# An expert layer whose VectorE instructions read the gathering tokens and a list of indices from PSUM, with fewer PSUM banks for the first products

## The reference, cut to what matters

```python
def block(hb):                       # 128 tokens
    q = (hb @ wq).reshape(128, 8, 2, 128)
    s = jnp.einsum('thsd,snd->thsn', q, subkeys)
    s1, i1 = lax.top_k(s[:, :, 0], 16)
    s2, i2 = lax.top_k(s[:, :, 1], 16)
    cand = (s1[..., :, None] + s2[..., None, :]).reshape(128, 8, 256)
    sc, ci = lax.top_k(cand, 16)
    e1 = jnp.take_along_axis(i1, ci // 16, axis=-1)
    e2 = jnp.take_along_axis(i2, ci % 16, axis=-1)
    idx = e1 * 128 + e2              # 16384 experts
    gate = jax.nn.softmax(sc, axis=-1)
    u_sel, v_sel = u_tab[idx], v_tab[idx]
    act = gelu(jnp.einsum('td,thkd->thk', hb, u_sel)) * gate
    return jnp.einsum('thk,thkd->td', act, v_sel)
```

## Time and profile before

| | us |
|---|---|
| median of 3 runs | 4457.77 (4456.28 to 4461.15) |
| span of the profiled execution | 4448.2 |
| median less span | 9.6 |
| PE busy | 4243.8 (95%) |
| DVE busy | 3101.9 (70%) |
| ACT busy | 1806.5 (41%) |
| POOL busy | 1550.2 (35%) |

### The profile page before, as it was taken

How to read it: one execution, slowest core, us unless ns; L and a number is a source line. 1 busy time by engine, 2 the same in 40 slices (tenths; PEclk the granted TensorE clock), 3 DMA queues, 4 the chain that set the end, 5 groups by cost and what they waited for, 6 DMA issues and landing times.

```text
span 4448.2 us, 66516 instructions
## 1 busy us (share of the span) xinstructions
PE 4243.8 (95%) x26227; PEld 3699.9 (83%) x26227; DVE 3101.9 (70%) x4740; ACT 1806.5 (41%) x2814; POOL 1550.2 (35%) x1005
## 2 busy tenths in 40 slices
PE   7979989999989999999999999999999999999998
PEld 5857745779989999999989877699889877877997
DVE  5866667559878988788878555588478544555873
ACT  4245411233334544333345335455255333323542
POOL 2044224215887657777721110211111110112121
PEclk8989999999999999999999999999999999999999
DMA  4133522224875779999933322133323332102332
GB/s 180 53 105 124 182 69 70 80 89 157 260 247 199 271 287 393 376 382 388 366 108 105 95 87 66 48 105 96 100 91 105 95 104 77 47 34 68 103 99 75
DMA packets 232190, 665.74 MB, mean 150 GB/s; under 512 B 22519, under 2 KB 88455, under 8 KB 229704
## 3 DMA queue, kind: packets, MB, share of 16 engines
q1 hardware_dynamic: 110528, 389.87, 26.1%
q0 software_dynamic: 38752, 142.90, 8.8%
q10 hardware_dynamic: 82600, 128.71, 8.1%
HBM read 593.24 MB, written 68.16 MB: 149 GB/s over the span
## 4 chain that ended last, share of the span: by engine, by line
PE 74%; DVE 16%; POOL 3%; ACT 3%; issue 3%; DMA 1%; ACTq 0%; DVEq 0%; POOLq 0%
PE ps L271 14%; PE ps L272 14%; PE ps L273 14%; PE ps L2727 5%; PE ps L2729 5%; PE ps L2728 5%; DVE r L240 2%; PE ps L1611 2%; DVE A L2042 2%; PE ps L3762 1%; PE ps L1690 1%; DVE A L2341 1%; POOL r L240 1%; DVE A L2342 1%; DVE r L290 1%
## 5 line engine op out<-in xcount | busy, mean ns | idle before, releaser
L271 PE MATMUL ps<-r,r 128*128 128x384 f32 (+1 forms) x3944 | 1454.4, 369 | 22.2 <-POOL r L240 14.6
L272 PE MATMUL ps<-r,r 128*128 128x384 f32 (+1 forms) x3944 | 1436.3, 364 | 0.0
L273 PE MATMUL ps<-r,r 128*128 128x384 f32 (+1 forms) x3944 | 1435.8, 364 | 0.0
L240 DVE TENSOR_TENSOR r<-A,r 128x1024 fp32r<-128x1024 f32 x436 | 603.9, 1387 | 718.7 <-ACT r L234 713.0
L234 ACT ACTIVATE r<-A 128x1024 fp32r<-128x1024 f32 x513 | 542.2, 1058 | 1200.9 <-PE ps L273 995.3
L271 PEld LDWEIGHTS ps<-r,r 128*128 128x128 f32 x3944 | 745.6, 189 | 118.7 <-issue 24.5
L272 PEld LDWEIGHTS ps<-r,r 128*128 128x128 f32 x3944 | 745.7, 189 | 81.5 <-issue 3.4
L273 PEld LDWEIGHTS ps<-r,r 128*128 128x128 f32 x3944 | 745.2, 189 | 81.6
L287 ACT ACTIVATE r<-A 128x512 fp32r<-128x512 f32 (+1 forms) x796 | 474.1, 611 | 503.4 <-DVE A L2415 233.5
L2727 PE MATMUL ps<-r,r 128*128 128x256 f32 x2128 | 601.0, 282 | 3.5 <-DVE A L2891 2.5
L2729 PE MATMUL ps<-r,r 128*128 128x256 f32 x2128 | 600.4, 282 | 0.0
(11 more groups left out here) (532 smaller groups left out, 5544.8 us busy)
## 6 DMA issues: line engine op xcount, KB each, us to landing
A<-in_pu SPq DMA_DIRECT2D x128, 512.0 KB
A<-in_pv SPq DMA_DIRECT2D x128, 512.0 KB
A<-in_f1i SPq DMA_DIRECT2D x88, 512.0 KB, 3.5
A<-in_f2i SPq DMA_DIRECT2D x88, 512.0 KB, 3.6
A<-in_w_in SPq DMA_DIRECT2D x48, 512.0 KB
acts<-A ACTq DMA_DIRECT2D x128, 192.0 KB
gates<-A ACTq DMA_DIRECT2D x8, 3072.0 KB, 11.3
A<-gates ACTq DMA_DIRECT2D x32, 768.0 KB
```

What stands on the lines that cost most here:

```text
L240: e.tensor_tensor(self.vr(at + 1024, 1024), self.v(self.st0 + 1024 * (u % RS), 1024), self.vr(at, 1024).bitcast(F32), ALU.subtract).then_i ...
L271: t.matmul(o, hi, xh, start=first and k == k0, stop=False)
L272: t.matmul(o, hi, xl, start=False, stop=False)
L273: m = t.matmul(o, lo, xh, start=False, stop=final and k == K - 1)
```

## The change

The gathering tokens stay in banks 6 and 7, where the transposes left them (the two are now one tensor of 1024 columns, `last2`), and DVE reads them there for rows 0 to 95 (`L.kept`). From row 96 on it reads the copy in SBUF as before, since vexp 6 and 7 want the banks: PE waits for row 95 before vexp 6. The transposes of the gates move from banks 6 and 7 to 3, 4 and 5, which need a wait for the last scores. Early products use banks 0, 1, 2 up to c = 69 and from there only 0 and 1 in turn. After the GELU of c = 70 ACT copies the list of indices into bank 2, and `hot_v` reads it there. In tiles and sizes nothing else changes.

```diff
-        self.PS = [ctx.enter_context(nc.psum_tensor(f"ps{i}", [128, 512], F32)) for i in range(8)]
+        self.PS = [ctx.enter_context(nc.psum_tensor(f"ps{i}", [128, 512], F32)) for i in range(6)]
+        self.last2 = ctx.enter_context(nc.psum_tensor("ps67", [128, 1024], F32))
+        self.PS += [self.last2[:, 0:512], self.last2[:, 512:1024]]
...
+        L.THREE = 70
...
+        L.bank = [c % 3 if c < L.THREE else (c + 1) % 2 for c in range(128)]
         for b in range(3):
-            self.plan([("early", c) for c in range(b, 128, 3)] + [("vsum", b)] + ([("sum t", b)] if b < 2 else []), (b,))
-            self.plan([("gates", i) for i in range(b, NT // 4, 3)] + [("vsum", 3 + b)], (3 + b,))
-        self.plan([("x tokens", 0), ("gate t", 1), ("gate t", 3), ("vsum", 6)], (6,))
-        self.plan([("x tokens", 1), ("gate t", 2), ("vsum", 7)], (7,))
+            self.plan([("early", c) for c in range(128) if L.bank[c] == b] + [("vsum", b)] + ([("sum t", b)] if b < 2 else []), (b,))
+        for b in range(3):
+            self.plan([("gate t", b + 1)] + [("gates", i) for i in range(b, NT // 4, 3)] + [("vsum", 3 + b)], (3 + b,))
+        for i in range(2):
+            self.plan([("x tokens", i)], (6 + i,))
+            self.plan([("vsum", 6 + i)], (6 + i,))
...
+        L.kept = L.steps["second", 4].stop
...
-                v.scalar_tensor_tensor(out=row, in0=row, scalar=1.0, in1=self.v(L.XT, 1024), op0=ALU.mult, op1=ALU.mult,
+                tokens = self.last2[:, :] if n < L.kept else self.v(L.XT, 1024)
+                v.scalar_tensor_tensor(out=row, in0=row, scalar=1.0, in1=tokens, op0=ALU.mult, op1=ALU.mult,
...
+                t.wait_ge(*S.at("out", "scores", 15))
                 ps = self.bank_t(t, "gate t", tt)
...
+            if c == L.THREE:
+                a.wait_ge(*S.at("out", "early", c - 2))
+                a.activation(self.PS[2][:, 0:128], self.cst("iota128"), ACT.Copy).then_inc(*S.on("a", "iota kept"))
...
-            io = self.cst("iota128").unsqueeze(1).to_broadcast([128, 8, 128])
+            io = self.PS[2][:, 0:128].unsqueeze(1).to_broadcast([128, 8, 128])
...
+        v.wait_ge(*S.at("iota kept"))
         v.wait_ge(*S.at("out", "gate t", 3))
...
+            if x == 6:
+                t.wait_ge(*S.at("row used", L.kept - 1))
```

## The result

| | us |
|---|---|
| before, median of 4 runs | 4457.02 (4451.72 to 4461.15) |
| changed, median of 4 runs | 4426.84 (4425.38 to 4446.54) |
| ratio | 0.994, 95% interval 0.9916 to 0.9963 |
| changed once more, median of 6 runs | 4430.25 (4425.62 to 4440.89), ratio 0.9939 (0.9919 to 0.9959) |

What follows compares the result with a forecast made beforehand. PE sets the end; POOL and DVE hold each other up when DVE reads two SBUF operands, and DVE limits the gates stage. 4457.8 - 12.2 - 9.7 + 1.6 + 0.4 = 4437.9 us; range 4429 to 4451.

Steps and rivals of the forecast that it cites:

- C: Rival: the change does not free POOL and DVE at this size, only costs are left; 4460 us, chance 0.07.
- A: Rival: POOL's gathers are slow for another reason, half the top-k gain goes; 4444 us, chance 0.10.
- B: Rival: DVE remains the limit in the gates stage, half of that gain; 4443 us, chance 0.12.
- D: Rival: weights late with two banks, GELUs hold PE in early 114 to 127; 4468 us, chance 0.07.
- both main terms: The gains from PE's shorter waits in the top-k stage (12.2 us) and the gates stage (9.7 us).
- a clock that would come back behind the large gap: Top-k stage: full clock would return another 3.4 us (17% of 20 us); counted only in the range's lower end.
- top-k stage: Rows read from PSUM let POOL keep pace; PE's 18.0 us of waits fall to 5.75, gain 12.2 us.
- gates stage: List and rows from PSUM make PE the limit; its 17.5 us of waits fall to 7.8, gain 9.7 us.
- wait at vexp 0: Early 127 and vexp 0 share bank 0, so PE waits for the GELU; cost 1.6 us.
- two banks: From c = 71 PE waits for the GELU of c - 2; cost 0.4 us, bounds 0 and 6.
- waits for ACT's copies: Gates stage: of 3.0 us of such waits 2 stay, since they hang on ACT's order.
- first gap: Start of the gates stage: PE stands 7.25 us behind POOL's remainder and first product; 5.8 us are left.

Runs made afterwards that it cites:

- both_sbuf: The changed kernel, with rows 0 to 95 and the comparisons reading tokens and list from SBUF again; 4456.88 us, ratio 0.9999 to the kernel before.

## Why the prediction was right

**The direction and the mechanism** held, each step of it. An instruction with one PSUM input was not held (the 96 rows took 1199 to 1222 ns), as L1642 had let expect. The table of the Trainium skill, "VectorE: DVE Perf Modes", section on the TRN2 errata, with its dearer PSUM input, is not borne out at 1024 columns either, for instructions with one input in PSUM and one in SBUF: 1.21 us, as with both in SBUF where nothing holds them. both_sbuf rules out that anything else made the gain. Against C: these rows and the comparisons were not held. Against A: gathers beside them went to 0.95 us. Against B: DVE left its limit. Against D: no GELU held PE in early 114 to 127.

**The size** came out larger: -19.9 forecast, by the layer's times -30.45 + 1.58 = -28.9 us. The ratio times the first median of before gives 4431 us, inside the range; the median itself, 4426.84, lies 2 us under its lower end, the second series' 4430.25 inside. So the range was met at its edge, and partly by luck: both main terms lie beyond their own bounds (13.3 and 11.7), and the end at 4429 was reached with 3.4 us for a clock that would come back behind the large gap. That gap stayed, and so did its low clock (0.93 in the 20 us). Term by term:

| term | forecast | measured |
|---|---|---|
| top-k stage | -12.2 | -15.15 |
| gates stage | -9.7 | -15.3 |
| wait at vexp 0 | +1.6 | +1.58 |
| two banks | +0.4 | 0 (0.4 with two banks throughout) |

What the sum lacked is the price of a stop. I had counted a wait at its recorded length and left the clock alone. In the top-k stage I had left 5.75 us of waits; 6.8 were left, the large one with 4.72 against 4.75. The waits of PE fell by 11.0 us, but the time by 15.15. The traces give three parts for the other 4.2 us, all estimates.

The first is the clock behind the large gap: 5 us at 0.50 before, 2.5 us lost, against 1.7 us in the changed kernel, so 0.8 less. The prediction's 3.4 us for that clock was too much: it counted 17% of 20 us, in a part of which PE stood. The second is the small stops, at full clock. Here is the first of them in the kernel before, with PE's matmuls around it, and the clock of the stretch that holds it:

```profile
1152.96 0.34 PE L272 MATMUL ps<-r,r 128*128 128x384 f32 x1
1153.13 0.34 PE L273 MATMUL ps<-r,r 128*128 128x384 f32 x1
1154.39 0.42 PE L271 MATMUL ps<-r,r 128*128 128x384 f32 x1 [0.93 <-POOL r L240]
1154.65 0.34 PE L272 MATMUL ps<-r,r 128*128 128x384 f32 x1
...
1130.00:1257.00 127.00, 118.74 (x663) 115.52 (x662) 94.20 (x128) 43.77 (x60) 107.09 (x50) 1.00 0.79 255
```

A matmul is recorded with 0.34 us, yet the next one starts 0.17 to 0.18 us behind it. Across the stop the starts lie 1.26 and then 0.26 us apart, 1.17 us more than the usual 0.35 for two, for a wait recorded with 0.93. So this stop cost 0.24 us more than its recorded wait, with the clock at 1.00 all the time. If each does, 8 fewer stops (5 small ones left of 13) make 1.9 us. The third part is five delays in the kernel before that are recorded with 0.03 to 0.06 us and lost some 0.28 each, 1.4 us.

In the gates stage, of the 5.6 us that I missed 2 are the waits for ACT's copies. I kept them as ACT's order; they went, all 3.0 us, so they were a consequence of late one-hot blocks. The other 3.6 us are again more time than recorded wait (11.7 us of waits, 15.3 of time). The clock is hardly in it: 0.64 before and 0.67 after in the 5 us behind the first gap, and 1.00 from 1386 to 1630 us, where the others lie. The seven smaller stops of before, at 0.24 each, would make 1.7 us. For the rest I have no recorded wait. The first gap came out as said, 5.68 against 5.8.

The slack of DVE was right in kind: 49.7 us of idle before its remainders, which take 1.64 us (I had taken 2.0).

## What to carry to other kernels

Where VectorE and GpSimd work side by side, look for VectorE instructions with two SBUF operands in the timeline: if their durations have two values (1.21 and 2.9 or 3.4 us here), one operand that is read often and stays the same belongs in PSUM, if a bank can be spared; check what the banks' next users wait for. Instructions that keep two SBUF inputs keep the trouble (gathers of 2.8 us beside the search here). When waits of TensorE are removed, expect more than their recorded length: here 0.24 us for each short stop, and 1.6 to 1.7 us behind gaps of 4.7 and 5.7 us, where the granted clock fell. Behind such a change the remaining gaps are places in the hand-written orders (an exponential three products too late, a product behind four gathers), and each is worth a look at what stands ahead of the late instruction in its queue.

## What the runs showed of the hardware

A gather instruction on GpSimd took 0.95 us beside one-input or PSUM-reading work of VectorE, 1.76 us in the median beside work with two SBUF inputs in the top-k stage, and 2.83 us at most. The Trainium skill, "SBUF — State Buffer", practical consequences, infers that a `tensor_tensor` leaves descriptor generation alone. For these gathers, whose indices lie in SBUF, the rows say otherwise: in the changed kernel the gather at 1212.18 us took 2.83 us beside a `tensor_tensor` with two SBUF inputs, and 0.95 us beside PSUM-reading rows. Whether it is held in reading the indices or in writing descriptors, no run tells. Beyond that, a gap of 4.7 to 5.7 us on TensorE was followed by granted clocks of 0.83 to 0.93 in a stretch of 20 us, and without the gap it was 1.00; stops of 0.9 to 1.6 us between 1130 and 1257 us left it at 1.00.
